# Gated linear attention in chunks: state product ahead of the next chunk's level products on TensorE, state update ahead of the mask on VectorE

## The reference, cut to what matters

```python
def step(state, inp):                       # one chunk of one head
    qi, ki, vi, gi = inp
    b = jnp.cumsum(gi, axis=-2)
    o_inter = jnp.einsum('bhck,bhkv->bhcv', qi * jnp.exp(b), state)
    ...                                     # a: causal products q k^T with decay
    o = o_inter + jnp.einsum('bhij,bhjv->bhiv', a, vi)
    b_last = b[..., -1, :]
    state = jnp.exp(b_last)[..., None] * state + jnp.einsum(
        'bhck,bhcv->bhkv', ki * jnp.exp(b_last[..., None, :] - b), vi)
    return state, o
```

## Time and profile before

| | us |
|---|---|
| median of 3 runs | 5881.75 (5880.16 to 5884.71) |
| the profiled execution | 5878.97 |
| its span, first to last instruction | 5877.1 |
| TensorE busy in the span | 4739.7 (81%) |
| VectorE busy | 2483.6 (42%) |
| this stage, first exponential to the next stage's start | 3411.55 to 3992.20, 580.65 |

### The profile page before, as it was taken

The page is one execution under the profiler, slowest core; times in us unless marked ns, Lnnn a source line. Parts: engine busy times, 40 slices in busy tenths (PEclk is TensorE's granted clock), DMA queues, the critical chain, the costliest instruction groups (busy, mean ns, idle before and its releaser), DMA issues. The chain is left out here.

```text
span 5877.1 us, 60726 instructions
## 1 busy us (share of the span) xinstructions
PE 4739.7 (81%) x23305; PEld 3695.0 (63%) x23305; DVE 2483.6 (42%) x3030; ACT 1608.2 (27%) x2461; POOL 757.9 (13%) x674
## 2 busy tenths in 40 slices
PE   6996399779828979999999968865777835699798
PEld 3883256268515658888888758754666712478676
DVE  3121676241167731111111167795555446433333
ACT  2120155131115521111111144433333223222222
POOL 1001200010030010000000022351222234100100
PEclk8998599989959989999999979977888967799899
DMA  4343201332320023223222111111000044122222
GB/s 152 107 140 116 90 26 44 112 115 93 119 98 26 36 98 102 98 86 106 95 97 96 65 46 53 56 50 43 29 17 27 8 174 149 61 88 84 82 93 86
DMA packets 243311, 479.26 MB, mean 82 GB/s; under 512 B 30968, under 2 KB 66140, under 8 KB 242732
## 3 DMA queue, kind: packets, MB, share of 16 engines
q1 hardware_dynamic: 241632, 471.57, 23.5%
q0 software_dynamic: 1488, 5.11, 0.3%
HBM read 362.33 MB, written 114.29 MB: 81 GB/s over the span
## 5 line engine op out<-in xcount | busy, mean ns | idle before, releaser
L519 DVE TENSOR_TENSOR p_wl<-p_raw,p_wh 128x2048 fp32r<-128x2048 f32 x96 | 220.0, 2292 | 798.3 <-ACT p_wh L460 798.3
L460 ACT CAST p_wh<-p_raw 128x2048 fp32r<-128x2048 f32 x96 | 183.6, 1912 | 833.7 <-PE p_ps L370 828.4
L370 PE MATMUL p_ps<-p_wh,him 128*128 128x512 f32 x1024 | 401.4, 392 | 8.1 <-POOL lom L503 4.1
L370 PE MATMUL p_ps<-p_wl,him 128*128 128x512 f32 x1024 | 400.3, 391 | 0.0
L370 PE MATMUL p_ps<-p_wh,lom 128*128 128x512 f32 x1024 | 400.2, 391 | 0.0
L523 DVE COPY p_stg<-p_ps 128x512 f32<-128x512 f32 x168 | 115.9, 691 | 632.6 <-PE p_ps L370 610.6
L370 PE MATMUL p_ps<-p_wh,hi 128*128 128x512 f32 x896 | 353.9, 395 | 16.5 <-DVE p_wl L519 8.4
L370 PE MATMUL p_ps<-p_wl,hi 128*128 128x512 f32 x896 | 352.0, 393 | 0.0
L370 PE MATMUL p_ps<-p_wh,lo 128*128 128x512 f32 x896 | 351.8, 393 | 0.0
L370 PE MATMUL p_ps<-him,p_wh 128*128 128x512 f32 x768 | 298.8, 389 | 0.0
L370 PE MATMUL p_ps<-him,p_wl 128*128 128x512 f32 x768 | 298.8, 389 | 0.0
(11 more groups left out here) (397 smaller groups left out, 10286.1 us busy)
## 6 DMA issues: line engine op xcount, KB each, us to landing
p_raw<-w_in SPq DMA_DIRECT2D x96, 1024.0 KB, 5.7
pn_dram<-p_stg SPq DMA_DIRECT2D x128, 256.0 KB, 2.0
u_raw<-w_up SPq DMA_DIRECT2D x32, 1024.0 KB, 5.5
u_raw<-w_down SPq DMA_DIRECT2D x32, 1024.0 KB, 4.9
p_dram<-p_stg SPq DMA_DIRECT2D x112, 256.0 KB, 2.0
m_w<-w_mod SPq DMA_DIRECT2D x12, 2048.0 KB, 8.1
pt_dram<-p_stg SPq DMA_DIRECT2D x96, 256.0 KB, 2.0
d_raw<-pt_dram SPq DMA_DIRECT2D x24, 512.0 KB, 4.6
```

Of the source, the lines that this page charges most:

```text
L370: mm = pe.matmul(ps[:, u, :], lhsT, rhs, start=(kk == 0 and q == 0), stop=(kk == KD - 1 and q == 2))
L460: act.copy(wh[:, kh], raw[:, kh]).then_inc(s_wh[kh], 1)
L519: dve.tensor_tensor(wl[:, kh], raw[:, kh], wh[:, kh], ALU.subtract).then_inc(s_wl[kh], 1)
```

## The change

On TensorE P(m) with its waits goes ahead of A(m+1); the order is now P(m), A(m+1), O(m). On VectorE U(m) with its wait goes ahead of M(m+1); the order is now U(m), M(m+1), preparation steps. No instruction is added or taken away, and ScalarE, GpSimd and the SP queue keep their programs.

```diff
@@ VectorE @@
             mask(0)
             for m in range(M):
                 n, c = at(m)
-                if m + 1 < M:
-                    mask(m + 1)
                 dv = width(n)
                 if c < UPD:
                     dve.wait_ge(s_S, upd(m) + 1)
@@
                         dve.scalar_tensor_tensor(nxt, S[:, c % 2, 0:dv], el[:, n % 2, c:c + 1], pS[:, 0:dv], ALU.mult, ALU.add).then_inc(s_Sc, 1)
+                if m + 1 < M:
+                    mask(m + 1)
                 if n + 1 < H:
                     for s in spread.get(c, ()):
                         prepare(n + 2, s)
@@ TensorE @@
                 b, sl, dv = n % 2, slice(c * CK, (c + 1) * CK), width(n)
-                if m + 1 < M:
-                    ahead(m + 1)
                 if c == 0:
                     pe.wait_ge(s_v[b], 16 * (n // 2 + 1))
                 if c < UPD:
@@
                     pe.matmul(pS[:, 0:dv], kd[:, m % 2], v[:, b, c, 0:dv], start=True, stop=True).then_inc(s_S, 1)
+                if m + 1 < M:
+                    ahead(m + 1)
                 if m >= 2:
                     pe.wait_ge(s_oc, m - 1)
```

## The result

The changed kernel takes 5895.28 us (median, 5891.66 to 5898.54), the kernel before 5881.14 (5873.91 to 5888.13) beside it: a ratio of 1.0024, with an interval of 1.0015 to 1.0032. It is slower by 14 us, where 4.3 were forecast. The time lies in the range of 5874 to 5898, but near its upper end: it is closer to the rivals "one more collision" (5898) and "the lower clock" (5901) than to the forecast of 5886.1, and it is slower by over 0.2%, an outcome that the prediction had given 0.17.

A forecast was written before the change was run, and what follows sets the result against it. Branch a was read as VectorE's burst then a TensorE chain, branch b as close to VectorE-bound. Terms 4.6 + 2.0 - 1.8 - 0.5 gave +4.3 us, median 5881.75 to 5886.1; range 5874 to 5898.

The forecast's parts named there:

- one more collision: Rival: GpSimd's later start stretches one more VectorE step a head, 1.07 us each, giving 5898; chance 0.12.
- the lower clock: Rival: one more TensorE group in each branch a head's tail runs at the lower clock, 15 us, giving 5901; chance 0.08.
- What bounds the stage: Branch a heads: VectorE's burst to U(4) or U(5), then a TensorE chain; branch b close to VectorE-bound; waits at P no price.
- Run-ahead for mask, +0.77 a head: Branch a, heads 0 to 5: TensorE loses 1.90 us of run-ahead, an earlier U saves the mask's 1.13: +0.77 us a head.
- holds nothing: Branch a tail: U(5) is done by about 3617.8, before P(6) starts at 3618.80, so it delays nothing.
- Collisions "no net effect": Port shared by VectorE and GpSimd: the 1.0 us shift re-deals collisions, taken as no net effect.
- The bound I gave: Collisions: one more or one less a head, 1.07 us times 11, 12 us either way.
- The sign that I had named for being wrong: VectorE's burst from step 0 to U(5) changing by over 1 us would show the prediction wrong.
- The delay of K(2): P(2) waits 1.0 us for its copy, delaying GpSimd's start; costs +1.0 us each in heads 6 and 7.
- at the stage's start: P(0) stands at K(0) with A(1) behind it, but O(0) waits 11.7 us for the first mask anyway: nothing.
- the only sign of that kind: K being waited for in chunks other than 2 would show the prediction wrong.
- Branch b and the end: Heads 8 to 10: earlier U(5) shortens M(0)'s wait, -0.6 us each; head 11's end: state part of O(7) hides, -0.5.

The follow-up runs named there:

- e6: The changed kernel with each of GpSimd's products cut to 16 columns (output not the reference's): 5790.85 us, ratio 0.9839 to the kernel before.
- e5: The kernel before with each of GpSimd's products cut to 16 columns (output not the reference's): 5792.48 us, ratio 0.9842.
- e4: The changed kernel with 16 throwaway products on TensorE ahead of P(5)'s wait in heads 0 to 7: 5880.24 us, ratio 0.9994 to the kernel before.
- e7: The kernel before with throwaway products on TensorE: 12 ahead of P(5) in heads 0 to 7, 10 ahead of P(6) in heads 8 to 10: 5875.50 us.
- e11: The changed kernel with 14 throwaway products ahead of P(3)'s wait in the heads of branch a, none ahead of P(5): 5888.52 us, ratio 1.0011.
- e3: The changed kernel with the copy K(2) taken inside ScalarE's step 0, so that P(2) no longer waits for it: 5894.52 us, ratio 1.0026.
- e1: The kernel before with only VectorE's half of the change, U(m) ahead of M(m+1), TensorE keeping its order: 5879.52 us, ratio 0.9992.
- e10: The kernel before with throwaway products: 12 ahead of P(5) in heads 0 to 5, 10 ahead of P(6) in heads 8 to 10: 5872.53 us.

## Why the prediction was right or wrong

**What bounds the stage: right.** The wait at P was not the price. Its total hardly moved (115.4 for 111.7 us) while the kernel grew slower by 14 us.

**Run-ahead for mask, +0.77 a head: right in kind and nearly in size.** P(6) to the next step 0 grew by 1.83 a head in heads 0 to 5, forecast 1.79; step 0 to U(2) fell by 1.21, forecast 1.13. e6 against e5 gives +0.61 a head where nothing else disturbs it, e4 against e7 +3.0 for seven heads.

**The clock, put at nothing: the step that failed.** I took the lower clock for a rival at 0.08 with the argument that "the idle time per head hardly changes". The wait that matters did change: ahead of P(5) heads 0 to 6 wait 17.2 us in total before and 34.5 after. In most of these heads it is a wait of 5.3 us, behind which A(6) and not only P(5) and O(5) stands. P(5) to P(6) at full clock is 4.02 us before and 4.13 after by the working; seven heads should take 28.1 and 28.9 and took 37.1 and 43.0, 9.0 us more before and 14.1 more after: +5.1. Not all of the 9.0 and 14.1 can be had back by a better clock, since P(6) also waits for U(5), about 4.8 us behind P(5); that U(5) "holds nothing" was right only behind a slow stretch. Most of the growth in this part is the rival's mechanism at a third of its price, for I had put a whole group's 1.90 on each of 8 heads, where part of the slow stretch was there before and VectorE's way to U(5) covers some of it. e4 shows it (-9.85 us in that part, A(6) from 3.19 to 1.73), e11 that a fill two chunks ahead doesn't do it. By the Trainium skill ("TensorE: Matmul & The Clock Gate", Why this matters for your kernels), which asks to avoid idle gaps between bursts, this case was to be likelier; the trace agrees with it at P(5), 3.19 us for 1.73 behind a gap of 5.34.

**Collisions "no net effect": half right.** In heads 0 to 5 U(2) to U(4) grew by only 1.5 us. Head 6 is where it failed: its U(2) to U(4) went from 12.10 to 15.48 us. Before, it had the fewest collisions of all, but waited for GpSimd at its end, and that wait is gone: P(6) to step 0 fell from 18.80 to 16.96. With P(5) to P(6) up by 1.47 the head lost 1.79 instead of 1.0. The bound I gave, 12 us either way, was fair: e11 moved 5.3 us of them with 14 products on TensorE, by way of O(3). The sign that I had named for being wrong, a burst from step 0 to U(5) changed by over 1 us, shows in head 6 (27.69 us for 24.52). In heads 0 and 5 it is 1.2 us shorter, which is the mask's 1.13 that the forecast itself takes off; in heads 1 and 2 it is 1.4 shorter, in heads 3 and 4 0.2.

**The delay of K(2): there, and its price wrong.** P(2) waits 0.86 us for it (forecast 1.0). It was to cost 1.0 in heads 6 and 7 through GpSimd. Head 7 became 0.70 us shorter, and e3, without the delay, is no faster. Of the 13 waits for K, eleven are P(2)'s (0.22 to 0.87 us, in branch b 1.56 to 1.64); one of 6.20 us is at the stage's start, where O(0) waits longer for its mask, as the prediction said; and one, 0.76 us at 3792.70, is in another chunk, the only sign of that kind.

**Branch b and the end: near in size, by another path, and eaten elsewhere.** VectorE's last idle time before the next head's U(0) is 0.72 us instead of 1.51, but it stands ahead of M(7) and not of M(0):

```profile
3869.60 1.22 DVE L1562 TENSOR_TENSOR g_am<-g_pa,g_masks 128x1024 f32<-128x1024 f32 x1 [0.72 <-PE g_pa L1617]
```

From U(5) to the next head's U(0), with the masks between counted alike, that is -0.8 us, forecast -0.6. That it comes so near is in part luck. M(7) waits for A(7), which takes 3.4 us here (3865.98 to 3869.39) where I had 2.5, while P(6) and O(6) together take 1.4 instead of 2.69; and M(0) then follows M(7) on VectorE without a wait. But U(2) to U(4) of head 8 grew by 0.7, from 20.10 to 20.80, and the head won 0.13. In head 10 one more collision between U(4) and U(5) (9.17 us for 8.09) turns a forecast gain into +0.66. At the end the state part of O(7) hides, as forecast; the last product then waits for the sum of the levels and runs at half speed, 1.22 us for the 0.59 of the kernel before:

```profile
3999.91 0.61 PE L1640 MATMUL g_po<-g_S,g_X 128*128 128x256 f32 x2
4002.86 1.22 PE L1649 MATMUL g_po<-g_v,g_AT 128*128 128x256 f32 x2 [2.33 <-DVE g_AT L1565]
```

The end itself is worth 0.4 us (from the start of the last reduction to the next stage 6.18 us before, 5.81 after), forecast 0.5.

**The sum.** The forecast missed the stage by 6.5 us: heads 0 to 5 by 5.1 (3.8 of it P(5) to P(6), 1.1 the way to U(4), 0.2 behind P(6)), head 6 by 0.8, head 7 by -1.7, heads 8 and 9 by 0.5, the rest by 1.8. The direction came from the terms that held. A clock term put at nothing and collisions that mostly fell the wrong way make the distance from 4.3 to 10.8. The other 3.3 us up to the median's 14 lie outside the stage or in the scatter of executions; the interval of the ratio, 8.8 to 18.8 us, holds 10.8 and not 4.3. That the time still lies in the range is owed to the range's width, which was meant for collisions.

**What stays open.** The clock's return behind the same wait of 5.34 us isn't the same in each head: P(5) to P(6) is 5.56 us in head 6 and 6.96 in head 3. No run tells what decides it. Nor was a version tried that holds the collisions still while the wait is filled, so the shares of the two in e4's 12.0 us (9.85 and 4.21, less what the late P(5) takes) are readings of one trace. Nor was one tried that fills both P(3)'s and P(5)'s wait, though e11 shows that the first deals collisions. What moves the collisions of the kernel before into those of e1 and of the kernel after was not taken apart further.

## What to carry to other kernels

A wait in the list is a price only if what is behind it is late; but the products right behind it can run at the lower clock. If an order of work moves a group of matmuls from ahead of a wait to behind it, count the group at the lower clock, unless another wait ends the stretch anyway. Where an engine must wait ahead of a chain that sets the end, throwaway products in the wait can pay: 15 us in the kernel after (e4), 9 in the kernel before (e10). A slow group that looks harmless, since another engine sets the time, can still shift what a third engine starts (e11). And where two engines collide at every second instruction, a shift of a microsecond anywhere moves the time by some microseconds; put it in the range rather than in the sum.

## What the runs showed of the hardware

VectorE's 0.68 us steps take 1.5 to 2.9 us when GpSimd works beside them, and the whole of what GpSimd's products do in this kernel is some 90 us: cut to 16 columns, they take it from 5883.58 to 5792.48 us. I had expected 60 to 80.

The granted clock behind a wait depends on what TensorE did right ahead of it: in head 3, 14 extra products two chunks earlier leave the group behind the wait at 3.19 us, though they raise the mean clock of heads 0 to 6 from 0.90 to 0.95; 16 in the wait itself bring it to 1.73.
